# A two-model forward pass in fp32 on one core: early turns, meta norm, last copy and decay gate in other orders; last tokens packed; value products by pairs of steps

## What is computed

```python
# layer 0: differential attention; layer 1: neighbourhood attention, 16 heads of width 64
a = softmax(q k^T + bias);  o = a @ v          # 256 tokens by 256 tokens for each head
# third block
h = concatenate([meta, x])                      # 272 tokens
xn = rms_norm(h, norm_mix_g)                    # the meta rows are normed too
q, k, v, f_logit, b_gate, c_gate, u = split(xn @ w_in)
log_f = log_sigmoid(f_logit + b_f);  cum = cumsum(log_f)      # the decay gate
s = q k^T * 64**-0.5 + cum[query] - cum[key]    # causal
y_attn = softmax(s) @ v                         # 8 heads of width 64
y_conv = b_gate * causal_depthwise_conv(c_gate * u, conv_w)
y = concatenate([head_rms_norm(y_attn), head_rms_norm(y_conv)])   # squares summed over 64 features
h = h + y @ w_out                               # then a feed-forward part and the final norm
```

## Time and profile before

| | |
|---|---|
| median of 3 runs | 996.93 us (996.74 to 998.97) |
| the profiled execution | 997.15 us, span of its instructions 995.3 us |
| PE busy | 984.1 us, 99% of the span |
| VectorE, ScalarE, GpSimd busy | 644.9, 506.2, 131.6 us |
| granted TensorE clock, mean | 0.998 of full |
| the chain that ended last | PE 95%, DVE 3%, ACT 1%, DMA 1% |

### The profile page before, as it was taken

How to read it: one execution, slowest core, us unless ns; L and a number is a source line. 1 busy time by engine, 2 the same in 40 slices (tenths; PEclk the granted TensorE clock), 3 DMA queues, 4 the chain that set the end, 5 groups by cost and what they waited for, 6 DMA issues and landing times.

```text
span 995.3 us, 14663 instructions
## 1 busy us (share of the span) xinstructions
PE 984.1 (99%) x5874; PEld 858.4 (86%) x5874; DVE 644.9 (65%) x1015; ACT 506.2 (51%) x751; POOL 131.6 (13%) x207
## 2 busy tenths in 40 slices
PE   8999999999999999999999999999999999999997
PEld 8999788888888898888888888889889999999995
DVE  6878776555556887656755555578665967545554
ACT  7676654444445565645534344465654455344442
POOL 2300995900000000000000000013600000000000
PEclk9999999999999999999999999999999999999999
DMA  9954579856554574334755555545543338555511
GB/s 292 255 197 139 146 170 221 275 174 205 176 193 162 169 247 136 105 108 148 239 185 195 186 184 197 174 175 169 191 144 111 111 109 285 173 190 191 184 71 43
DMA packets 113668, 174.78 MB, mean 176 GB/s; under 512 B 6152, under 2 KB 74768, under 8 KB 113600
## 3 DMA queue, kind: packets, MB, share of 16 engines
q1 hardware_dynamic: 107168, 165.43, 52.0%
q0 software_dynamic: 6272, 8.15, 3.5%
q10 hardware_dynamic: 160, 0.27, 0.1%
HBM read 172.77 MB, written 1.05 MB: 175 GB/s over the span
## 4 chain that ended last, share of the span: by engine, by line
PE 95%; DVE 3%; ACT 1%; DMA 1%; issue 0%; SPq 0%
PE bank L1051 29%; PE bank L1052 28%; PE bank L1053 28%; PE bank L1173 2%; PE bank L1066 1%; PE bank L1203 1%; DVE wl L1591 1%; PE bank L1294 1%; PE bank L1233 1%; PE bank L1239 1%; PE bank L1227 1%; PE bank L1183 1%; DMA h<-in_x_dram 1%; PE bank L1206 0%; DVE v_reg L1644 0%
## 5 line engine op out<-in xcount | busy, mean ns | idle before, releaser
L1591 DVE TENSOR_TENSOR wl<-raw,wh 128x2048 fp32r<-128x2048 f32 x152 | 348.8, 2302 | 172.9 <-ACT wh L626 172.8
L626 ACT ACTIVATE wh<-raw 128x2048 fp32r<-128x2048 f32 x152 | 288.0, 1909 | 107.7 <-PE bank L1053 107.7
L1051 PE MATMUL bank<-wh,xh 128*128 128x512 f32 (+2 forms) x664 | 250.2, 377 | 0.0
L1052 PE MATMUL bank<-wl,xh 128*128 128x512 f32 (+2 forms) x664 | 245.3, 369 | 0.0
L1053 PE MATMUL bank<-wh,xl 128*128 128x512 f32 (+2 forms) x664 | 245.2, 369 | 0.0
L1051 PE MATMUL bank<-xh,wh 128*128 128x256 f32 (+1 forms) x672 | 194.8, 290 | 0.2
L1052 PE MATMUL bank<-xl,wh 128*128 128x256 f32 (+1 forms) x672 | 190.4, 283 | 0.0
L1053 PE MATMUL bank<-xh,wl 128*128 128x256 f32 (+1 forms) x672 | 190.4, 283 | 0.0
L1053 PEld LDWEIGHTS bank<-wh,xl 128*128 128x128 f32 (+1 forms) x664 | 124.4, 187 | 22.2
L1051 PEld LDWEIGHTS bank<-wh,xh 128*128 128x128 f32 (+1 forms) x664 | 124.4, 187 | 22.0 <-issue 1.4
L1052 PEld LDWEIGHTS bank<-wl,xh 128*128 128x128 f32 (+1 forms) x664 | 124.6, 188 | 20.2
(11 more groups left out here) (257 smaller groups left out, 880.3 us busy)
## 6 DMA issues: line engine op xcount, KB each, us to landing
raw<-in_w_ff_dram SPq DMA_DIRECT2D x32, 1024.0 KB, 5.3
raw<-in_ffn_w_gate_dram SPq DMA_DIRECT2D x44, 512.0 KB, 4.0
raw<-in_ffn_w_up_dram SPq DMA_DIRECT2D x44, 512.0 KB, 5.0
raw<-in_ffn_w_down_dram SPq DMA_DIRECT2D x22, 1024.0 KB, 5.0
raw<-in_na_w_qkv_dram SPq DMA_DIRECT2D x12, 1024.0 KB, 5.1
raw<-in_w_in_dram SPq DMA_DIRECT2D x12, 1024.0 KB, 5.2
raw<-in_da_w_qkv_dram SPq DMA_DIRECT2D x8, 1024.0 KB, 10.2
raw<-in_ple_w_gate_dram SPq DMA_DIRECT2D x8, 1024.0 KB, 5.0
```

Of the source, the lines that this page charges most:

```text
L626: nc.scalar.activation(wh[:, i % RING, :], raw[:, i % RAW, :], ACT.Copy).then_inc(s_hi, 1)
L1051: nc.tensor.matmul(dst, lh, rh, start=start, stop=False, skip_group_check=True)
L1052: nc.tensor.matmul(dst, lh, rl, start=False, stop=False, skip_group_check=True)
L1591: nc.vector.tensor_tensor(wl[:, i % RING, :], raw[:, i % RAW, :], wh[:, i % RING, :].bitcast(F32), ALU.subtract).then_inc(s_lo, 1)
```

## The change

- **Early turns:** `first_turns` is called for k = 0, 1 ahead of the 8 warm-up transposes and for k = 2, 3 behind them.
- **Meta norm:** VectorE does it a slot earlier (`META_SLOT - 3`).
- **Last copy:** in ACT's `tail_0`, `copy_turned(0, 15)` comes ahead of the second half of the value squares and of `last_values(0)`.
- **Value products by pairs, layer 1:** PE does those of steps i-1 and i together at odd i, with 256 columns for each matmul instead of 128. Even steps have none, and valued goes up by 2.
- **Last tokens packed, third block:** high and low part of the last 16 tokens lie side by side in `x_last` (32 columns, one copy each by ACT and VectorE), and are the weights of one matmul with the high part of `w_in`, so the low-by-high product lands in 16 rows of its own. Each k takes two matmuls instead of three. Keys 16 to 31 of the last chunk then stand for the same tokens again, so ACT copies 16 probability columns at each odd step (with a wait on its own exponential ahead), and the root columns get 16 more.
- **Decay gate:** on VectorE the split of the second-to-last unit ahead of the f chain goes behind the chain's first part.
- **Convolution squares:** each product of `y_sq` with `head_ones` becomes two, with 64 weight columns into 64 partitions each.

```diff
-            nc.scalar.activation(prob_2(s, n), ..., ACT.Exp, ...).then_inc(exped.sem, 1)
+            ins = nc.scalar.activation(prob_2(s, n), ..., ACT.Exp, ...)
+            if b == 1:
+                link(ins)
+                flat = prob_2(s, 384)
+                ins = nc.scalar.activation(flat[:, T:T + META], flat[:, S:T], ACT.Copy)
+            ins.then_inc(exped.sem, 1)
...
                 copy_turned(0, 14)
+                copy_turned(0, 15)
                 value_squares(2, (1,))
                 last_values(0)
-                copy_turned(0, 15)
                 last_values(1)
...
+            wait(act, turned_hi, "mix2", 1, 1)
+            nc.scalar.activation(x_last[:, :, 0:META], xh[:, :, XP - META:XP].bitcast(F32), ACT.Copy).then_inc(s_last, 1)
             split_to(u + 5)
...
+                    if b == TB:
+                        pe.wait_ge(s_last, 2)
+                        for k in range(4):
+                            nc.tensor.matmul(banks[b][0:2 * META, :], x_last[:, 4 * kh + k, :], w_hi[:, k, :], ...)
+                            ins = nc.tensor.matmul(banks[b][0:META, :], x_last[:, 4 * kh + k, 0:META], w_lo[:, k, :], ...)
...
-                if 0 <= i < 16:
+                if 0 <= i < 16 and not (l == 1 and i % 2 == 0):
...
-                                dst = value_bank(i // 4)[64 * m:64 * m + 64, S * (g % 2) + P * b:S * (g % 2) + P * b + P]
+                                dst = value_bank(i // 4)[64 * m:64 * m + 64, S * (g % 2):S * (g % 2) + S]
                                 ins = nc.tensor.matmul(dst, v_s[:, kb, P * g + 64 * m:P * g + 64 * m + 64],
-                                                       pt[:, b, 256 * m + P * kb:256 * m + P * kb + P],
+                                                       pt[:, :, 256 * m + P * kb:256 * m + P * kb + P],
...
-                    ins.then_inc(valued.sem, 1)
+                    ins.then_inc(valued.sem, 2 if l == 1 else 1)
...
-                    first_turns(0)
+                    first_turns(0, (0, 1))
                     for _ in range(WARM[1]):
                         nc.tensor.transpose(bank[0][:, 0:P], ident[:, :], ident[:, :])
+                    first_turns(0, (2, 3))
...
-                                ins = nc.tensor.matmul(bank[4][:, 8 * b + 2 * m:8 * b + 2 * m + 2],
-                                                       y_sq[:, m, b * P:(b + 1) * P], head_ones[:, :], start=True, stop=True)
+                                for half in range(2):
+                                    at = b * P + 64 * half
+                                    ins = nc.tensor.matmul(bank[4][head_rows(half), 8 * b + 2 * m:8 * b + 2 * m + 2],
+                                                           y_sq[:, m, at:at + 64], head_ones[:, :], start=True, stop=True)
...
-                    if l == 0 and slot == META_SLOT - 2:
+                    if l == 0 and slot == META_SLOT - 3:
                         meta_norm()
...
-            split_to(first["in", "k"] + 2 + 3)
+            wait(dve, turned_lo, "mix2", 1, 1)
+            nc.vector.tensor_copy(x_last[:, :, META:2 * META], xl[:, :, XP - META:XP].bitcast(F32)).then_inc(s_last, 1)
+            split_to(first["in", "k"] + 2 + 2)
             dve.wait_ge(s_fdone, 1)
...
-            nc.vector.tensor_copy(r_keys[0:META, 2:3], bank[3][0:META, T + 2:T + 3]).then_inc(s_rkeys, 1)
+            nc.vector.tensor_copy(r_keys[0:2 * META, 2:3], bank[3][0:2 * META, T + 2:T + 3]).then_inc(s_rkeys, 1)
+            split_to(first["in", "k"] + 2 + 3)
             dve.wait_ge(s_fe, 1)
```

More of the change, by code:

```diff
@@ L693, in spread_root @@
                 wait(act, r_spread, name)
+                if name == "mix2":
+                    nc.scalar.activation(r_cols[:, T:T + META], src[:, S - META:S], ACT.Copy)
                 nc.scalar.activation(r_cols[:, META:T], src[:, 0:S], ACT.Copy).then_inc(r_ready.sem, 1)
@@ L1084, in tokens_unit @@
                         need(name, b, kh)
[L1085 to L1091 removed]
+                    if b == TB:
+                        pe.wait_ge(s_last, 2)
+                        for k in range(4):
+                            nc.tensor.matmul(banks[b][0:2 * META, :], x_last[:, 4 * kh + k, :], w_hi[:, k, :],
+                                             start=kh == first_kh and k == 0, stop=False, skip_group_check=True)
+                            ins = nc.tensor.matmul(banks[b][0:META, :], x_last[:, 4 * kh + k, 0:META], w_lo[:, k, :],
+                                                   start=False, stop=kh == last_kh and k == 3, skip_group_check=True)
+                    else:
+                        for k in range(4):
+                            if name == "att1" and k % 2 == 0:
+                                need(name, k // 2, kh)
+                            ins = three(banks[b][0:c.stop - c.start, :], x_of(4 * kh + k, c), (w_hi[:, k, :], w_lo[:, k, :]),
+                                        kh == first_kh and k == 0, kh == last_kh and k == 3)
+                            if fine and k < 3:
+                                yield
                     if b == len(cols) - 1:
@@ L1122, in first_unit, with first_turns @@
                         norm_turn(name, spots.index(at), 1)
-            def first_turns(c):
-                for k in range(4):
+            def first_turns(c, ks=range(4)):
+                for k in ks:
                     if k % 2 == 0:
@@ L1498, in _ @@
             wait(pe, r_ready, "mix2")
[L1499 removed]
+            for c, n in enumerate((P, P, 2 * META)):
                 nc.tensor.matmul(bank[3][0:n, T + c:T + c + 1], r_cols[:, P * c:P * c + n], ident[:, 0:1], start=True, stop=True)
```

31 lines of the change are left out of this document (12 added, 19 removed).

## The result

The changed kernel takes 991.01 us (990.93 to 991.16, 4 runs), the kernel before took 997.59 in the four runs beside it: ratio 0.9938, 95% interval 0.9927 to 0.995. By the ratio that is 6.2 us less, where 4.0 were forecast. On another chip the two kernels came out at 0.9935 (0.9921 to 0.9949).

What follows compares the result with a forecast made beforehand. PE's work and waits were taken to bound the kernel. Terms of -0.6, -0.6, -0.5, -0.95, -0.86 and -0.48 summed to -4.0 us, giving 992.9 from the median 996.93, said as 993.0; range 991.4 to 994.9.

Steps and rivals of the forecast that it cites:

- What bounds the kernel: Whole kernel: PE's work and waits set the end, PE being busy 984.1 of 995.3 us.
- rival 4: Layer 1's value pairs: later products lay bare ScalarE's copies and cost what they save; mostly 994.0 us, chance 0.10.
- rival 1: Third block: the decay chain moves by 1.8 or more, so all of -1.85 comes out; 992.0 us, chance 0.12.
- stand in POOL's shadow: Third block: decay-chain operations with SBUF operands still wait for POOL's scalings, so the chain moves only 0.75 to 0.8 us.
- The new wait of 1 us: Third block: PE waits about 1 us ahead of the first transposes, released by ScalarE's exponential; a sign to check.
- rival 2: Convolution squares: halves of the array don't overlap, so their -0.48 is gone; 993.5 us, chance 0.12.
- rival 5: Program start: the clock rises later and the first product runs at the lower level; up to 1000.2 us, chance 0.03.
- The sum: Whole kernel: the six terms add to -4.0 us, giving 992.9 against the median, said as 993.0.

Runs made afterwards that it cites:

- lower group: Shorter runs of one kernel: the kernel before 996.3 to 997.2 us (14 runs), the changed kernel with early turns undone 990.7 to 991.0 (5 runs).
- upper group: Longer runs of one kernel: the kernel before 998.2 to 999.0 us (11 runs), the changed kernel with early turns undone 992.8 (1 run), the changed kernel none.

## Why the prediction was right, and where it was not

**What bounds the kernel, meta norm, last copy.** Right: every us came out of PE's work (3.9) or PE's waits (2.1), and the two orders gave 0.51 and 0.52 where 0.6 and 0.5 were worked out. PE's last product in layer 0's tail waits 0.27 for the copy that was named.

**Value products by pairs: the term that was mis-sized most,** -0.95 forecast and -2.68 found. The step that failed is "a step's value product of eight 128-column records took 0.59; a pair took 1.18". That counts from the first record to the next instruction's start. It leaves out the 0.17 us ahead of the group in which the weight loads stand, which the earlier trace rows show (0.17 before L1233, released by "issue"). The other part is the comparison: a wide group takes 1.01 from its first record to the next instruction (382.79 to 383.80), not the 1.06 of the score products. So a pair gives 1.18 - 1.01 + 0.17 = 0.34 us and not 0.12. No cost came with it: rival 4's wait did not appear.

**Packed tokens and decay gate:** -0.86 forecast, -1.48 found, near rival 1's time though not quite its -1.85. The failed step is that the chain's operations "stand in POOL's shadow", with POOL's end taken as fixed ("POOL's 7.1 us stand as before"). POOL's end moved, since the split that was put behind the stall had itself been among the scalings and held them up by 2.0 to 2.2 us. The port rule of the Trainium skill ("SBUF — State Buffer", "Who interferes with whom") had been cited for what POOL does to VectorE, and not for what VectorE does to POOL. The new wait of 1 us, named as a sign that would make the prediction wrong if absent, is absent; PE's starts show 0.3.

**Convolution squares:** right in size by luck, for two wrong reasons that cancel: 0.9 in PE's list, cut to 0.48 by VectorE. PE's own list gives only 0.52, since the narrow loads are again a visit: the stretch falls from 787.25 - 785.54 = 1.71 to 1.03, and the gap ahead of it grows by 0.16. That VectorE's roots would limit the gain was wrong: nothing waits for them. That halves of the columns overlap, which rival 2 denied with the rule of the Trainium skill ("TensorE: Matmul & The Clock Gate", Part 3, "What overlaps and what doesn't"), holds: pairs start 0.007 us apart, though both use all rows. Here the measurement decides against the rule.

**Early turns:** -0.6 forecast, -0.27 between the two profiles, and in the runs of the lower group nothing (990.7 to 991.0 without the edit, 990.7 to 991.3 with it). The first product began at 7.78 and not at 7.28. The step that failed is to take one profile's arrival of x (6.75; 5.79 and 6.26 in two others) and one profile's 0.10 a transpose for fixed: in the profile after they took 0.21, and it was they and not x that held the second pair. What the edit may do besides is to keep the upper group away, in which the kernel before spent 11 of 25 runs; the counts above point that way and don't prove it. If so, rival 5 had the sign wrong, since the idle time would be the risk and not what fills it.

**The sum.** From PE's starts the change gives 5.98 us. Against the lower group of before (median 996.65) the medians give 5.6, which is what the five terms behind the start add to (5.71). The rest of the 6.2 and 6.5 in the ratios is the upper group. So the forecast was short by two terms, pairs (1.73) and packing with the gate (0.62), less what the early turns didn't give.

## What to carry to other kernels

Read the cost of a group of narrow products by leaving one out, or from the last wide instruction ahead of it to the second behind it, against a group of full width in the same place: here 0.33 of 0.77 us belonged to the visit, and gathering visits paid nearly three times what the matmul counts promised. Where VectorE and GpSimd both work on SBUF, add up the large operations of both from first to last; here the order within moved the end by 0.2 us at most, and taking one split out of the stretch by 2. Two edits that each shorten one of two equal paths must be tried together: alone they gave 0.04 and 0, together 1.48. A kernel whose runs fall into groups must be compared group by group.

## What the runs showed of the hardware

- Going from weight loads of 128 columns to loads of 64 and back cost TensorE 0.33 us a visit; the loads stood still for 0.17 us ahead of the first narrow one and for 0.17 behind the last. Between the same neighbours, loads of 128 columns had no pause.
- GpSimd's four scalings (10.1 us) grew by 2.0 to 2.2 us for each VectorE split among them, in either order.
- Two products with full rows and 64 columns each ran side by side, 0.007 us apart, a pair each 0.058; separated by order they overlapped in part (1.34 us for 32 against 1.03).
- The moment at which TensorE's transposes go from 0.21 to 0.11 us each (1.2 to 2.4 GHz) differed between executions of the same start: by 4.9 us in two profiles, at 7.3 or later in three others, with the granted clock shown as 1.00 throughout.
